# The order of three loads on SyncE's queue while the samples attend

## What is computed

```python
for l in range(DEPTH):                                   # DEPTH = 2
    ...                                                  # input projection, prompt attention, mLSTM
    past = cache_nsa_kv[page_table, :, l].reshape(DB, P, 4, NSA_KV_HEADS, NSA_HD)
    a_s, rows_s, wbuf_s = nsa_sample(q, kvp, gt, pos_s, past, cache_win_kv[l], ...)
    ...
    xp = xp + jnp.concatenate([a_p, b_p], axis=-1) @ w_out[l]
    xs = xs + jnp.concatenate([a_s, b_s], axis=-1) @ w_out[l]
    ...                                                  # memory attention, MLP

# in nsa_attend, for the samples: three attentions, weighted by gates
s_c = jnp.einsum('btghd,bcgd->btghc', qg, kc) * scale    # compressed keys
...                                                      # their probabilities choose 8 blocks of 64 keys
s_s = jnp.einsum('btghd,bgtkd->btghk', qg, ks) * scale   # keys of the chosen blocks
s_w = jnp.einsum('btghd,bwgd->btghw', qg, kw) * scale    # the last 512 cached keys (the window)
o = g[..., 0:1] * o_c + g[..., 1:2] * o_s + g[..., 2:3] * o_w
```

## Time and profile before

| | before |
|---|---|
| median of 3 executions | 2598.32 us (2593.63 to 2603.81) |
| profiled execution: time / span on the core | 2600.5 us / 2598.8 us |
| mean granted TensorE clock | 0.940 |
| TensorE busy | 2371.0 us, 91% of the span |
| VectorE / ScalarE / GpSimd busy | 33% / 19% / 6% |
| DMA | 237.27 MB, mean 91 GB/s |

### The profile page before, as it was taken

One profiled execution on the slowest core, in us unless ns is written; L12 is line 12 of the kernel. 1 busy time (PEld: TensorE's weight loads), 2 busy tenths in 40 slices (PEclk: granted clock), 3 DMA queues, 4 the chain that ended last, 5 costly groups with the idle time before them and its releaser, 6 DMA issues. The chain is left out here.

```text
span 2598.8 us, 32013 instructions
## 1 busy us (share of the span) xinstructions
PE 2371.0 (91%) x11130; PEld 1502.7 (58%) x11130; DVE 854.9 (33%) x2258; ACT 502.3 (19%) x1202; POOL 154.0 (6%) x277
## 2 busy tenths in 40 slices
PE   6999999979577999999979999999795689999997
PEld 5746767545245888544366457765453468884443
DVE  2534444943353111000035434368333531110000
ACT  1302322630121111000032023236302221110000
POOL 0001113200000000000000001232000000000000
PEclk9999999889778999999989999988897689999999
DMA  5112242245204122210031223422461042112200
GB/s 211 68 65 91 82 130 84 76 162 218 74 9 162 65 76 87 79 65 33 0 151 68 71 96 89 124 84 64 162 227 65 9 166 93 65 65 79 71 27 41
DMA packets 81196, 237.27 MB, mean 91 GB/s; under 512 B 13721, under 2 KB 56026, under 8 KB 70562
## 3 DMA queue, kind: packets, MB, share of 16 engines
q1 hardware_dynamic: 62082, 180.08, 19.3%
q0 software_dynamic: 12544, 41.96, 5.1%
q10 hardware_dynamic: 6432, 13.36, 1.5%
HBM read 223.29 MB, written 20.40 MB: 94 GB/s over the span
## 5 line engine op out<-in xcount | busy, mean ns | idle before, releaser
L354 PE MATMUL ps<-hT,ring 128*128 128x272 f32 x2560 | 590.3, 393 | 0.9 <-DVE hT L513 0.9
L354 PEld LDWEIGHTS ps<-hT,ring 128*128 128x128 f32 x2560 | 487.3, 191 | 101.8 <-ACT hT L466 1.4
L2181 PE MATMUL ps<-ring,arena 128*128 128x512 f32 (+1 forms) x1280 | 472.4, 595 | 2.2 <-DVEq L241 2.2
L2181 PEld LDWEIGHTS ps<-ring,arena 128*128 128x128 f32 (+1 forms) x1280 | 200.1, 174 | 273.5 <-issue 273.5
L354 PE MATMUL ps<-ring,hT 128*128 128x512 f32 (+6 forms) x1216 | 333.1, 477 | 0.0
L354 PEld LDWEIGHTS ps<-ring,hT 128*128 128x128 f32 (+1 forms) x1216 | 168.8, 167 | 157.8 <-issue 147.7
L698 PE MATMUL ps<-ring 128*128 128x256 f32 x1024 | 253.0, 389 | 0.5 <-issue 0.5
L698 PEld LDWEIGHTS ps<-ring 128*128 128x128 f32 x1024 | 187.4, 192 | 48.2 <-issue 25.3
L567 DVE TENSOR_TENSOR x<-ps,x 128x512 f32<-128x512 f32 x32 | 22.1, 692 | 474.6 <-PE ps L2181 451.3
L2145 DVE TENSOR_SCALAR arena<-ps 128x272 f32<-128x272 f32 x64 | 28.3, 442 | 405.9 <-PE ps L354 405.9
L267 POOL DMA_DIRECT2D ring<-in_cx x128 | 68.9, 539 | 1428.6 <-issue 1428.6
(11 more groups left out here) (365 smaller groups left out, 2149.8 us busy)
## 6 DMA issues: line engine op xcount, KB each, us to landing
ring<-in_wst SPq DMA_DIRECT2D x50, 2048.0 KB, 8.7
ring<-in_cx SPq DMA_DIRECT2D x128, 128.0 KB
ring<-in_cx POOLq DMA_DIRECT2D x128, 128.0 KB, 2.3
ring<-in_kx POOLq DMA_DIRECT2D x128, 64.0 KB, 2.1
ring<-in_kx SPq DMA_DIRECT2D x128, 64.0 KB, 1.8
ring<-in_mkv SPq DMA_DIRECT2D x4, 2048.0 KB, 9.9
out_win_s<-in_win SPq DMA_DIRECT2D x16, 508.0 KB, 19.8
ring<-in_cT SPq DMA_DIRECT2D x2, 2048.0 KB, 7.6
```

Source lines behind the costliest of these rows:

```text
L354: ins = nc.tensor.matmul(bank[rows, 0:n], a, b, start=(m < groups), stop=(m >= len(mms) - groups))
L2181: ins = nc.tensor.matmul(ps[g * NS:g * NS + w, bank(half, t), :], hf[:, 8 * c + f, t * P:t * P + w], wt[:, f, :], start=(c == 0 and f < gr ...
```

## The change

`w_out` is split into two names of the table, and `win0` comes between them. The places in the ring stay as they were; they are now written out for eight names, since the formula counted positions. The wait on `kv_st` goes with `w_out1` alone, whose destination is the one that it guards. No instruction of another engine is moved.

```diff
-ORDER += ["k0", "k1", "k2", "k3", "w_out", "scores1", "win0", "v0", "v1", "win1", "v2", "v3"]
+ORDER += ["k0", "k1", "k2", "k3", "w_out0", "scores1", "win0", "w_out1", "v0", "v1", "win1", "v2", "v3"]
...
-    elif _n not in SLOT and _n != "w_out":
-        SLOT[_n] = (2, 0, 1, 3)[(_i - (_i > ORDER.index("w_out")) - ORDER.index("k0")) % 4]
+for _n, _at in (("k0", 2), ("k1", 0), ("k2", 1), ("k3", 3), ("scores1", 2), ("win0", 0), ("v0", 1), ("v1", 3)):
+    SLOT[_n] = _at
...
-        if n != "w_out":
+        if n[:5] != "w_out":
...
-            if n not in GATHERED and n not in ("w_out", "scores1"):
+            if n not in GATHERED and n not in ("w_out0", "w_out1", "scores1"):
...
-                if n == "w_out":
-                    sp.wait_ge(turned_free, 1)
-                    sp.wait_ge(ctp_st, 16)
-                    sp.wait_ge(kv_st, 16 * KV_STORES)
-                    for c in range(2):
-                        at, w = CH_AT[f"w_out{c}"]
-                        src = din["wst"][bass.ds(l, 1), at:at + P * w].rearrange("a (p w) -> (a p) w", p=P)
-                        if c == 0:
-                            sp.dma_start(ropf[:, 0:w], src).then_inc(w_out_ld[0], 16)
-                            continue
+                if n[:5] == "w_out":
+                    at, w = CH_AT[n]
+                    src = din["wst"][bass.ds(l, 1), at:at + P * w].rearrange("a (p w) -> (a p) w", p=P)
+                    if n == "w_out0":
+                        sp.wait_ge(turned_free, 1)
+                        sp.wait_ge(ctp_st, 16)
+                        sp.dma_start(ropf[:, 0:w], src).then_inc(w_out_ld[0], 16)
+                    else:
+                        sp.wait_ge(kv_st, 16 * KV_STORES)
                         src = src.rearrange("p (k n) -> p k n", k=KT)
                         sp.dma_start(z[:, 0:4, ZV:ZV + 512], src[:, 0:4]).then_inc(w_out_ld[1], 16)
                         sp.dma_start(z[:, 0:4, ZK:ZK + 512], src[:, 4:8]).then_inc(w_out_ld[1], 16)
```

## The result

The changed kernel takes 2589.5 us (median of 22 runs), the kernel before 2596.8 us (22 runs); the ratio is 0.9972, interval 0.9959 to 0.9985. That is a gain of 7.3 us (3.9 to 10.6), or 0.28%. The forecast was 20.8 us. The measured median lies within the range on record, but the gain is a third of the one forecast, and nearer to that of rival 1. Of the 23 executions of the kernel before with which experiments 1 to 4 are compared, one took 7074 us and is in no ratio.

What follows compares the result with a forecast made beforehand. TensorE's waits for `win0` in two layers, with the low clock behind them, were taken as the bound (22.96 us). Wait 14.9 us plus clock 5.85 us gave 20.8 us off, so 2579 us, range 2573 to 2591.

Steps and rivals of the forecast that it cites:

- the range on record: Predicted range of the changed kernel's time, 2573 to 2591 us, held at about 8 in 10.
- rival 1: `v0`'s gather shares turns with `win0` from 553.6; TensorE starts at 562.9, clock falls; gain 5 us, 2595 us; chance 0.15.
- The bound and its price: TensorE's waits for `win0` at half 0's window scores, plus the low clock behind them, cost 22.96 us over both layers.
- `win0` on an empty queue, 0.65 us of wait: Without 2 MB ahead, `win0` takes at most 9.1 us like `win1`, plus 0.5, leaving TensorE waiting 0.65 us per layer.
- The step that failed is that of the gather: 104 `win0` packets share with `v0`'s gather at 71 per us, adding 1.2 us at most; wait taken as 1.1 us.
- That packets already taken over go first: `win0` packets the DMA engines already hold precede the gather's: some 1188 of the 1292 left when `v0` is ready.
- from about 200 on: Number of `win0` packets left for `v0` to hinder from which the wait exceeds 3.3 us and the clock falls too.
- The clock: Behind the window scores' short wait of 1.1 us TensorE keeps full clock, giving back 2.84 and 3.01 us, together 5.85.
- `w_out1`, `v0`, `v1` and what follows: Loads issued or landing after `win0` are in before their first use, so TensorE does not wait for them; no cost.
- Rival 3: `w_out1`'s packets go among `win0`'s and the loads drain together: slower, about 2603 us, 2599 to 2606; chance 0.06.
- the bound of 3.3 us in the prediction: Gap of 3.3 us at line 1744, followed by clock 0.50; waits over 3.3 us were taken to drop the clock.

Runs made afterwards that it cites:

- experiment 1: Changed kernel with one more wait on GpSimd, so the gather of `v0` is not issued before `win0` has landed: 2573.3 us, ratio 0.9904.
- experiment 2: Kernel before, in its old order of loads, with the gather of `v0` held until `win0` has landed: 2589.3 us, ratio 0.9958.
- experiment 3: Changed kernel with `w_out1` issued only when `win0` has landed, the gather of `v0` left alone: 2589.1 us, ratio 0.9964.
- experiment 4: Changed kernel with the window's value rows laid out by the host in 2 KB runs, 1024 data packets in place of 2560: 2577.2 us, ratio 0.9904.
- experiment 6: Changed kernel with the first of `v0`'s two gather DMAs as it was, the second held until `win0` has landed: 2579.2 us, ratio 0.9932.
- experiment 5: Changed kernel with the gather of `v0` held until ScalarE has copied the first two `mix` tiles: 2577.4 us, ratio 0.9929.
- experiment 8: Kernel before, old order of loads, with eight filling steps of half 0 moved in front of the window scores: 2583.3 us, ratio 0.9945.

## Why the prediction was wrong, step by step

*The bound and its price* held. The waits for `win0` with the clock behind them were worth 23 us, and the versions without a wait gain 20 to 25.

*`win0` on an empty queue, 0.65 us of wait:* right in the main. With the gather held it is 0.94 and 0.79; the queue was not quite empty, since `w_out0` lands about 1 us after `win0` is issued (8.3 us after its own issue, 7.3 us ahead).

*The step that failed is that of the gather:* "The other 104 share with `v0`, at 71 per us: 1.5 us in place of 0.3 us. That adds 1.2 us at most". The count was nearly right: 82 short packets of `win0` were left at 558.6 us, when the gather had moved its first ten. Wrong was the division, twice. First, 71 per us is a mean over a stretch that has no one pace. In the kernel before, a third of the 425 packets of the earlier trace rows moved in the first half us (first line below, 556.5 to 557); from 557.5 to 562.5 us (the other two) it was 52 per us beside 48 of the gather, about one for one.

```profile
q1 hardware_dynamic: 143, 0.08, 53.8%
q0 software_dynamic: 238, 1.79, 86.4%
q1 hardware_dynamic: 260, 0.27, 15.5%
```

Second, and it matters more, both figures are for sixteen engines together, and the last packets were not spread over sixteen. In layer 1 of the changed kernel 126 of the 128 rises have come by 559.49, and the last two come at 562.36 and 564.62; in layer 2 the last eight come from 1845.63 to 1849.47. Each lagging engine had to fit up to 16 packets of the gather between its own. TensorE waits for the last of the 128 rises, so a mean over the engines says nothing on the end. Experiment 3 shows 8 and 26 packets per us in place of 71, experiment 6 that the delay goes with the length of the gather. It added 4.7 and 5.3 us, four times the "at most". Why some engines lag, and which, the traces do not tell. The Trainium skill, "DMA: Bandwidth & Descriptors", section "Latency and other measured facts", names two of the sixteen that are usually the slower ones. That would fit the two of layer 1 in experiment 3, and not the eight of layer 2.

That packets already taken over go first held: in the profile after q0 moves almost nothing until 558, over 4 us after its issue. It protected most of `win0`, but not the last packets of the laggards. Rival 1 was right in its mechanism, the turns, and wrong in when they begin. Its price, a wait of 5.85 us (562.9 − 557.05), came near the measured 5.6 and 6.1 in part by luck: it let 867 packets of `win0` follow the gather, while the last of them went beside it. Its condition, "from about 200 on", was taken from a sum over all engines too; some 80 were enough.

*The clock:* the wait came out at 5.6 and 6.1 us, so the clock fell, as rival 1 said. The loss was 1.42 and 2.41 us, not the 2.84 and 3.01 of before: the low stretch ends earlier, for a reason that no run isolates. For the short waits of experiments 1 and 5 (0.8 to 1.3 us) the step was right, no loss at all. The wait of 2.37 us in experiment 8 lost 1.8 us.

*`w_out1`, `v0`, `v1` and what follows:* right. No run has a wait for any of them. In experiment 1 `v0` is even issued 7 us later against `win0`, at no cost.

*Rival 3* (the loads drain together) is excluded by experiment 3.

## What to carry to other kernels

A load ends with its slowest DMA engine. If another queue's transfer sets in before the load is through on all of them, price it by that engine: each of its leftover packets waits for one of the other transfer's (0.31 us here), up to all that the other has on this engine (16, so 5 us), however few are left in sum. Before taking a load's time from a like load elsewhere, look for what else is issued within its age. If something is, hold it by a semaphore until the urgent load has landed, or make the urgent load's packets fewer and longer: with the better place in the queue each brought about 25 us here (19 to 31), where that place alone brought 7.

## What the runs showed of the hardware that was not expected

The clock did not depend on the length of a gap alone. A wait of 3.33 us in experiment 2 was followed by the full clock (line 1772 at 1.06 us), a wait of 3.34 us in experiment 6 by the low one (1.94 us), both in the same stage. In experiment 8 it fell behind a wait of 2.37 us. And the gap of 3.29 us in front of the short scores (line 1744 before, 1745 in experiment 1) is the same in every profile, but the clock behind it is not. The first line is experiment 1, the second the changed kernel, both of layer 1; PEclk is the third number from the end.

```profile
539.80:543.20 3.40, 3.39 (x64) 2.61 (x64) 1.05 (x5) 0.39 (x2) 0.00 (x0) 1.00 0.72 193
543.90:547.20 3.30, 3.30 (x39) 2.19 (x38) 1.34 (x6) 0.75 (x4) 0.00 (x0) 0.50 0.93 318
```

So the bound of 3.3 us in the prediction was no bound. The clock behind that earlier gap is in none of the sums of the table, and may be a part of what they miss.

Also, the length of the runs counted although the bytes are the same. In experiment 1, with 2560 data packets and no gather in flight, TensorE starts 556.29 − 546.39 = 9.9 us after the issue of `win0`, and waits for it. In experiment 4, with 1024, it starts 555.25 − 546.36 = 8.9 us after the issue, with the gather at its old place, and does not wait. About half of this us is the issue itself: the last of the eight DMAs is issued at 550.32 in experiment 1 and at 549.83 in experiment 4.
